# One 512-column product for the high and the low input, in the MLP and the retention query and key projections of a two-block network

## The chip, the core and the metric

The kernel runs on one core of one Trainium2 chip. The metric is the device time of one execution in microseconds; the median of a few executions is compared.

## The reference

The reference passes 256 tokens of width 1024 through two blocks. The first has an even layer (windowed attention with sinks, heads "A", and neighbourhood attention, heads "B"), an MLP, a retention layer (8 heads, decays in both directions, a group norm per head) and another MLP. An MLP is `square(relu(rmsnorm(x) @ w1)) @ w2` with 4096 hidden columns. The second block has causal, top-k and cross attention with gates; the keys and values of its cross attention come from a second input `mem` (256 rows). Everything is float32:

```
def _mlp(x, norm_g, w1, w2):
    h = _rmsnorm(x, norm_g)
    return jnp.square(jax.nn.relu(h @ w1)) @ w2
# retention, one direction
    a = jnp.einsum('bhid,bhjd->bhij', qc, kc) * dmask
    o = jnp.einsum('bhij,bhjv->bhiv', a, vc) + ...
    yn = (yf - mu) * lax.rsqrt(var + GN_EPS) * gn_g
```

## The kernel before

**Split products.** A float32 product is made of three products in the format `fp32r`: a high part times a high part, high times low, low times high (`mm3`, L382 to L384). For the weights, ScalarE (ACT) copies each half tile of the weights to its high part `whi` (L904), and VectorE (DVE) subtracts it from the raw tile to get the low part `wlo` (L1297). There are six `whi` and five `wlo` buffers and four raw tiles of 1 MB, filled by SyncE's queue (SP) in the order of `weight_tiles()`. Each engine casts a fixed number of halves ahead (`HI_AHEAD` 5, `LO_AHEAD` 4), at places in its program that `used(...)` fixes. Each engine runs its own program in a hand-written order, so an operation that waits holds all behind it.

**Two forms of product.** `n_half` holds the input (tokens) stationary and streams 512 weight columns. `t_half` holds a 128x128 block of weights stationary and streams the 256 tokens, so the result comes out transposed: for each of 8 k-blocks of one half tile there are three 256-column matmuls, `whi` with `hTh`, `whi` with `hTl`, `wlo` with `hTh`. One PSUM bank of 512 columns takes both halves of a tile. `t_first` does the same for the first tile of a stage, in two banks, with transposes of the second half of the input put between.

**Where `t_half` is used.** The MLP's first product ("w1", 16 tiles in each of 2 layers), the retention's queries and keys ("rq", 8 tiles), and, untouched by the change, "xk", "xq", the gates "gl" and the up products "wu".

**MLP.** In step j PE does the two halves of w1 tile j, and then tile j-1 of the second product (`acc_half`, L456: 24 matmuls of 512 columns into four banks). Between them stands a chain: ACT takes relu from the bank (L1104; L1109 for the two banks of tile 0), DVE squares (L1620), ACT copies the high part (L1114), DVE subtracts for the low part (L1622). PE waits for the last, one step later.

**Retention.** `hTh`, `hTl` are the gained but not yet row-scaled inputs. The row scale 1/rms(x) of queries and keys is spread over the partitions by a matmul with a matrix of ones (`broadcast("ret")`, L542) and multiplied in as DVE empties the banks (L1650, L1646). The group norm adds `GN_EPS` on GpSimd (POOL).

**The first stage (about the first 140 us).** The order of the weight tiles is qa, ka, qb, kb, memT (the transposed `mem`, split on the spot with its gain, L899 and L1290), vb, xk, xv, oe. Attention steps `att_step("AB", s)` for s from 0 to 18 are interleaved with the product halves: scores (L553), on DVE scores plus bias (L1396 for A) and row maxima, exp on ACT (L989), transposes (L565), copies (L1428 DVE, L1002 ACT), values (L582). Queries and keys are normed (`hn_squares`, `hn_sums`, `hn_scales` on POOL, `hn_scaled` L1325) and transposed (L525). Row squares of x (L913) and of `mem` are taken by ACT.

Of the kernel before, what the change touches and what calls it, by code (L numbers as in the profile page):

```python
# [25 lines left out]
C_ID, C_NA, C_CA, C_COS, C_SIN, C_U, C_L, C_IS, C_NS = (  # L26
    0, 128, 640, 896, 1024, 1152, 1536, 1920, 1928)
NCONST = 1936
# [6 lines left out]
        "w0", "w1", "w2", "w3", "w4", "raw0", "raw1", "raw2", "raw3", "x0", "x1", "t0", "t1", "t2", "t3", "t4", "id", "c", "g", "b", "m", "out"]  # L35
# [17 lines left out]
def weight_tiles():  # L53
# [86 lines left out]
def program(nc, A, out):  # L140
    with ExitStack() as st:
# [7 lines left out]
        hTh, hTl = sb("hTh", 2048, F32R), sb("hTl", 2048, F32R)  # L149
# [69 lines left out]
        hT = (v3(hTh, 8), v3(hTl, 8))  # L219
        ur = [(v3(h, 4, 0, 1024), v3(l, 4, 0, 1024)) for h, l in zip(urh, url)]  # L220
        ones, diag, rbc = cst[:, C_U:C_U + 128], cst[:, C_U + 128:C_U + 384], cst[:, C_L:C_L + 256]
        spread = {"mem": (av(EO, 128), av(ED, 256), av(EB, 256)), "ret": (ones, diag, rbc), "sec": (ones, diag, rbc)}
# [5 lines left out]
        invs, negs = cst[:, C_IS:C_IS + 8], cst[:, C_NS:C_NS + 8]  # L228
        skp, hb = lgt[:, 0:8], lgt[:, 8:32]
# [83 lines left out]
        def sp_program(e):  # L313
# [6 lines left out]
            for m, (label, name, k0, nk, c0, n, _) in enumerate(tiles):  # L320
# [22 lines left out]
                if m == 3:  # L343
                    e.dma_start(cst[:, 128:NCONST], A["consts"][:, 128:NCONST]).then_inc(S["c"], 16)
                    e.dma_start(rows[:, :], bass.AP(A["rowvec"].tensor, 0, [[0, 128], [1, NROW]])).then_inc(S["c"], 16)
# [14 lines left out]
        def pe_program(e):  # L360
# [64 lines left out]

            def t_first(label, stage, between):


                i = first_half[label]
                w2 = [weights(i), weights(i + 1)]  # L430
                o = [take("mm", label, m) for m in range(2)]
                for g in range(2):
                    for m in range(2):
                        h, l = w2[m]
                        for k in range(4 * g, 4 * g + 4):
                            w.wait_ge(*at(*x_split(stage, k)))
                            mm = mm3(o[m][:, 0:256], (h[:, k, :], l[:, k, :]), (hT[0][:, k, :], hT[1][:, k, :]),
                                     k == 0, k == 7)
                        if g == 0 and m == 0:
                            between()  # L440
                        if g:
                            mm.then_inc(*up("mm", ("mm", label, m), ("wd", i + m)))
                            give("mm", label, m)
# [199 lines left out]
            for s in range(19):  # L643
                if s == 0:
                    n_half("kb", 0, 512, "E")
                    value["wd", first_half["memT"]] = value["wd", first_half["memT"] + 1] = value["wd", first_half["kb"]]
# [5 lines left out]
                if s < 3:  # L652
                    n_half("kb", s + 1, 512, "E")
                if s == 3:
                    hn_transposed("qb")
                if s == 6:
                    hn_transposed("kb")
                if 3 <= s < 7:
                    n_half("vb", s - 3, 512, "E")
                if s == 7:  # L660
                    broadcast("mem")
# [7 lines left out]
                if s >= 15:  # L669
                    i, x = (s - 15) // 2, (s - 15) % 2  # L670
                    if s == 15:
                        acc_open("E")
                    w.wait_ge(*at("xl", "oe", i))
                    acc_half("E", ("oe", i), x, hT, 2 * i, start=s == 15)
            for i in range(2, 4):
                transposes(("oe", i), osb, 2 * i, [("o", "B", 0), ("o", "B", 1)])
# [6 lines left out]
            def mlp(layer, before):  # L683
                t_first(("w1", layer, 0), f"mlp{layer}", lambda: x_transposed(f"mlp{layer}", before, (2, 3)))
                for j in range(17):
                    if j == 1:
                        acc_open(f"mlp{layer}")
                    if 1 <= j < 16:
                        for x in range(2):
                            t_half(("w1", layer, j), x, 256, 8, hT, lambda k: x_split(f"mlp{layer}", k))  # L690
# [15 lines left out]
            for c in range(8):  # L706
                for x in range(2 if c else 0):
                    t_half(("rq", c), x, 256, 8, hT, lambda k: x_split("ret", k))
                if c == 1:
                    broadcast("ret")  # L710

            def ret_scores(h):
                b = take("rs", h)
                w.wait_ge(*at("rq", 7))
# [163 lines left out]
        def act_program(e):  # L878
# [31 lines left out]
            def row_squares(stage, src, junk, needs):  # L910
                for tb in range(2):
# [63 lines left out]
            def att_exp(key, i):  # L975
# [8 lines left out]
                for j, h in enumerate(hs):  # L984
                    if key == "A":
                        scl, nm = 2.0 ** -(h + 1), stats(("nm", "A", qb), 8)[:, h:h + 1]
# [18 lines left out]
            def att_step(key, s):  # L1005
# [3 lines left out]
                if key == "AB" and s in (6, 10):  # L1009
                    sink_exp((s - 6) // 4)  # L1010
                if s < n:
# [37 lines left out]
            used("qa", 2)  # L1049
# [11 lines left out]
            for s in range(19):  # L1061
                att_step("AB", s)
                if s < 3:
                    used("kb", s + 1)
                if s == 3:
                    hn_stored("qb")
                    hn_squares("kb")
                if s == 4:
                    row_squares("mem", osb, osb, [(S["m"], 16), (S["m"], 16)])
                if s == 6:  # L1070
                    hn_stored("kb")
                if 3 <= s < 7:
                    used("vb", s - 3)
                if s == 7:
                    v_stored("vb", 0, 512, bvv[:, 1, :], "E")
                    stored_broadcast("mem")
# [14 lines left out]

            def mlp(layer, gcol, before):
# [3 lines left out]
                for j in range(17):  # L1096
                    if j < 16:
# [4 lines left out]
                        if j:  # L1102
# [945 lines left out]
```

## Time and profile before

| | |
|---|---|
| time, median of 3 | 1023.01 us (1022.87 to 1023.74) |
| profiled execution, its own time | 1024.58 us |
| its span in the trace | 1022.8 us |
| PE busy | 1002.8 us (98%), 6194 matmuls |
| PE weight loads busy | 892.1 us (87%), 6194 loads |
| DVE busy | 648.6 us (63%) |
| ACT busy | 488.3 us (48%) |
| POOL busy | 137.8 us (13%) |
| mean granted TensorE clock | 0.999 |

Engines: PE is TensorE's matmuls, PEld its weight loads, DVE VectorE, ACT ScalarE, POOL GpSimd, SP SyncE. A matmul's duration in a row includes its way through the array and overlaps the next one's, so the pace of a stream is read from start to start.

### The profile page before, as it was taken

The page shows a single profiled execution, that of the slowest core. Times are in us where ns is not written, and L with a number is a line of the kernel's source. Part 1 is how long each engine was busy: PE and PEld are TensorE (multiplying, and loading weights), DVE is VectorE, ACT ScalarE, POOL GpSimd, SP SyncE. Part 2 cuts the span into 40 slices and gives each one's busy share as a digit, 9 for nine tenths or more (in the row PEclk, how much of TensorE's full clock was granted, in tenths as well). Part 3 has the DMA queues.
Part 4 walks back from the last instruction along what each step waited for, and adds up shares of the span by engine and source line. Part 5 has one row for each costly group of instructions (what it writes and reads, how often), then busy time and mean ns, then how long its engine had stood idle before and what let it go on. Part 6 is the DMA issues. An engine that isn't in the chain of part 4 may idle for free.

```text
span 1022.8 us, 15392 instructions
## 1 busy us (share of the span) xinstructions
PE 1002.8 (98%) x6194; PEld 892.1 (87%) x6194; DVE 648.6 (63%) x916; ACT 488.3 (48%) x746; POOL 137.8 (13%) x173
## 2 busy tenths in 40 slices
PE   8889999999999999999999999999999999999997
PEld 7668879999998998888889999999887889999995
DVE  4687756664555655666666554455767887657674
ACT  5575536444554533234545444454545445545452
POOL 0631004970000200110001000000550110000000
PEclk9999999999999999999999999999999999999999
DMA  9963345465456544335464456545544463354541
GB/s 343 295 206 124 103 145 165 171 207 199 165 190 211 176 166 165 124 124 206 165 206 163 167 178 215 183 166 172 197 168 141 133 190 124 124 165 125 173 157 42
DMA packets 106933, 174.82 MB, mean 171 GB/s; under 512 B 4080, under 2 KB 66672, under 8 KB 106864
## 3 DMA queue, kind: packets, MB, share of 16 engines
q1 hardware_dynamic: 106144, 173.01, 50.9%
q8 instruction: 50, 0.82, 0.3%
q10 hardware_dynamic: 720, 0.83, 0.2%
q14 instruction: 19, 0.16, 0.0%
HBM read 172.79 MB, written 1.05 MB: 170 GB/s over the span
## 4 chain that ended last, share of the span: by engine, by line
PE 91%; DMA 3%; DVE 3%; SPq 1%; issue 1%; POOL 1%; ACT 1%; DVEq 0%; POOLq 0%
PE ps L456 23%; PE ps L382 20%; PE ps L384 19%; PE ps L383 19%; PE ps L582 2%; DMA raw<-in_memT 2%; PE ps L553 1%; PE ps L508 1%; PE ps L728 1%; PE ps L565 1%; DMA raw<-in_w_in_e 1%; PE ps L716 1%; DVE wlo L1297 0%; DVE arena L1396 0%; PE ps L535 0%
## 5 line engine op out<-in xcount | busy, mean ns | idle before, releaser
L1297 DVE TENSOR_TENSOR wlo<-raw,whi 128x1024 fp32r<-128x1024 f32 x314 | 373.8, 1229 | 30.3 <-ACT whi L904 13.9
L904 ACT ACTIVATE whi<-raw 128x1024 fp32r<-128x1024 f32 x314 | 317.4, 1049 | 95.5 <-PE ps L384 50.5
L382 PE MATMUL ps<-hTh,whi 128*128 128x256 f32 (+1 forms) x872 | 249.1, 286 | 0.4
L384 PE MATMUL ps<-hTh,wlo 128*128 128x256 f32 (+1 forms) x872 | 246.8, 283 | 0.0
L383 PE MATMUL ps<-hTl,whi 128*128 128x256 f32 (+1 forms) x872 | 246.8, 283 | 0.0
L382 PEld LDWEIGHTS ps<-hTh,whi 128*128 128x128 f32 (+1 forms) x872 | 166.8, 191 | 3.9 <-issue 1.9
L383 PEld LDWEIGHTS ps<-hTl,whi 128*128 128x128 f32 (+1 forms) x872 | 166.8, 191 | 1.2
L384 PEld LDWEIGHTS ps<-hTh,wlo 128*128 128x128 f32 (+1 forms) x872 | 166.8, 191 | 0.0
L382 PE MATMUL ps<-whi,hTh 128*128 128x512 f32 (+1 forms) x376 | 150.7, 401 | 6.3 <-DVE wlo L1297 2.3
L384 PE MATMUL ps<-whi,hTl 128*128 128x512 f32 (+1 forms) x376 | 145.3, 386 | 0.0
L383 PE MATMUL ps<-wlo,hTh 128*128 128x512 f32 (+1 forms) x376 | 145.1, 386 | 0.0
L456 PE MATMUL ps<-whi,urh 128*128 128x512 f32 x328 | 102.1, 392 | 0.0
L456 PE MATMUL ps<-wlo,urh 128*128 128x512 f32 x328 | 101.6, 390 | 0.0
L456 PE MATMUL ps<-whi,url 128*128 128x512 f32 x328 | 101.5, 390 | 0.0
L1620 DVE TENSOR_TENSOR arena<-arena 128x512 f32<-128x512 f32 x32 | 22.8, 713 | 122.7 <-ACT arena L1104 122.4
L382 PEld LDWEIGHTS ps<-whi,hTh 128*128 128x128 f32 x376 | 70.8, 188 | 24.4 <-issue 7.5
L384 PEld LDWEIGHTS ps<-whi,hTl 128*128 128x128 f32 x376 | 70.8, 188 | 14.8
L383 PEld LDWEIGHTS ps<-wlo,hTh 128*128 128x128 f32 x376 | 71.0, 189 | 12.9
L1104 ACT ACTIVATE arena<-ps 128x512 f32<-128x512 f32 x30 | 17.9, 598 | 131.8 <-PE ps L384 131.8
L456 PEld LDWEIGHTS ps<-wlo,urh 128*128 128x128 f32 x328 | 61.6, 188 | 13.1
L456 PEld LDWEIGHTS ps<-whi,url 128*128 128x128 f32 x328 | 61.6, 188 | 13.0
L456 PEld LDWEIGHTS ps<-whi,urh 128*128 128x128 f32 x328 | 59.5, 189 | 10.4
(185 smaller groups left out, 1131.7 us busy)
## 6 DMA issues: line engine op xcount, KB each, us to landing
raw<-in_w SPq DMA_DIRECT2D x64, 1024.0 KB, 5.4
raw<-in_w_in SPq DMA_DIRECT2D x34, 1024.0 KB, 5.2
raw<-in_w_in_o SPq DMA_DIRECT2D x24, 1024.0 KB, 5.4
raw<-in_w_out_o SPq DMA_DIRECT2D x8, 1024.0 KB, 5.0
raw<-in_w_in_e SPq DMA_DIRECT2D x7, 1024.0 KB, 14.5
raw<-in_w_mem SPq DMA_DIRECT2D x4, 1024.0 KB, 7.0
raw<-in_w_out_e SPq DMA_DIRECT2D x4, 1024.0 KB, 4.9
raw<-in_w_out SPq DMA_DIRECT2D x4, 1024.0 KB, 5.2
```

Source lines behind the costliest of these rows:

```text
L382: e.matmul(o, a[0], b[0], start=start, stop=False)
L383: e.matmul(o, a[0], b[1], start=False, stop=False)
L384: return e.matmul(o, a[1], b[0], start=False, stop=stop)
L456: mm = e.matmul(bank("acc", stage, 2 * tb + i), x[p], t[p % 2][:, 0, 512 * i:512 * i + 512], start=start and p == 0, stop=stop and p == 2)
L508: mm = e.transpose(b[:, j * 256 + tb * 128:j * 256 + tb * 128 + 128], src[:, tb, (k0 + j) * 128:(k0 + j) * 128 + 128], ident)
L553: mm = e.matmul(b[:, j * 256:j * 256 + nk], q_of(h, qb), k_of(h, nk), start=True, stop=True)
L565: mm = e.transpose(b[:, (j * nb + kb) * 128:(j * nb + kb) * 128 + 128], P[:, j, kb * 128:kb * 128 + 128], ident)
L582: mm = e.matmul(b[:, h * hd:h * hd + hd], T[:, (j * nb + kb) * 128:(j * nb + kb) * 128 + 128], v_of(h, kb), start=kb == 0, stop=kb == nb - 1)
L904: e.activation(split_half(i)[0], raw_half(i), ACT.Copy).then_inc(*up("hi", ("hi", i)))
L1104: e.activation(rl, bank("mm", ("w1", layer, j), 0), ACT.Relu).then_inc(*up("aev", ("rl", layer, j), ("free", ("mm", ("w1", layer, j), 0))))
L1297: e.tensor_tensor(l, raw_half(i), h.bitcast(F32), ALU.subtract).then_inc(*up("lo", ("lo", i)))
L1620: e.tensor_tensor(sq, rl, rl, ALU.mult).then_inc(*up("dst", ("sq2", layer, j)))
```

## The change

1. `hTh` and `hTl` become one buffer in which, for each k-block, 256 high columns stand beside 256 low ones. In "w1" and "rq", `t_pair` replaces the two `t_half`: per k-block one matmul of `whi` with all 512 columns and one of `wlo` with the 256 high ones. Each half tile now fills a whole bank: columns 0 to 255 hold high times high plus low times high, 256 to 511 high times low.
2. ACT copies the right half of the bank out (`low_copied`), DVE adds the left half to it (`low_added`), for each half tile. In the MLP, relu and square become one DVE operation.
3. The retention's broadcast goes away. The keys' scale is applied as a per-row factor to the scores (`rk`), the queries' is left out, and the group norm's epsilon is scaled to match (`ge`).
4. The first stage is reordered: weight tiles vb before memT, `weights_to(6)` and the row squares of x ahead of weight halves 6 and 7, the rest of the constants and of the row vector loaded at tile 14 in place of tile 3, `mem`'s row squares one per step, its broadcast at s = 9, "xk" emptied at s = 10 and 12, the last two "oe" transposes at s = 18 inside the loop; `used(...)` before the norm work in DVE's and ACT's steps. The A heads' sink maximum and scale become one DVE operation in place of two.

```
-        hTh, hTl = sb("hTh", 2048, F32R), sb("hTl", 2048, F32R)
+        hTs = sb("hT", 4096, F32R)
+        h4 = hTs[:, :].rearrange("p (k s n) -> p k s n", k=8, s=2)
+        hT = (h4[:, :, 0, :], h4[:, :, 1, :])
...
+    rows_first("vb", "w_in_e", 1792, 512)
     rows_first("memT", "memT", 0, 256)
-    rows_first("vb", "w_in_e", 1792, 512)
...
-                if m == 3:
-                    e.dma_start(cst[:, 128:NCONST], A["consts"][:, 128:NCONST]).then_inc(S["c"], 16)
-                    e.dma_start(rows[:, :], ...).then_inc(S["c"], 16)
+                if m == 4:
+                    e.dma_start(cst[:, 128:C_COS], A["consts"][:, 128:C_COS]).then_inc(S["c"], 16)
+                    e.dma_start(rows[:, R_SINK:NROW], ...).then_inc(S["c"], 16)
+                if m == 14:
+                    e.dma_start(cst[:, C_COS:NCONST], A["consts"][:, C_COS:NCONST]).then_inc(S["c2"], 16)
+                    e.dma_start(rows[:, 0:R_SINK], ...).then_inc(S["c2"], 16)
...
+            def t_block(label, m, ks, stage):
+                i = first_half[label] + m
+                h, l = weights(i)
+                o = bank("mm", label, m)
+                for k in ks:
+                    w.wait_ge(*at(*x_split(stage, k)))
+                    both = hTs[:, k * 512:k * 512 + 512]
+                    if k == 0:
+                        e.matmul(o, h[:, k, :], both, start=True, stop=False)
+                    mm = e.matmul(o[:, 0:256], l[:, k, :], hT[0][:, k, :], start=False, stop=False)
+                    if k:
+                        mm = e.matmul(o, h[:, k, :], both, start=False, stop=k == 7)
+                if k == 7:
+                    mm.then_inc(*up("mm", ("mm", label, m), ("wd", i)))
+                    give("mm", label, m)
...
+            def low_copied(label, m, dst):
+                w.wait_ge(*at("mm", label, m))
+                e.activation(dst, bank("mm", label, m)[:, 256:512], ACT.Copy).then_inc(*up("aev", ("lc", label, m)))
...
+            def low_added(label, m, d):
+                w.wait_ge(*at("lc", label, m))
+                e.tensor_tensor(d, bank("mm", label, m)[:, 0:256], d, ALU.add).then_inc(
+                    *up("dev", ("t", label, m), ("free", ("mm", label, m))))
...
-                        e.tensor_tensor(sq, rl, rl, ALU.mult).then_inc(*up("dst", ("sq2", layer, j)))
+                        w.wait_ge(*at("t", ("w1", layer, j), 1))
+                        e.scalar_tensor_tensor(sq, rl, 0.0, rl, ALU.max, ALU.mult).then_inc(*up("dst", ("sq2", layer, j)))
...
-            used("qa", 2)
+            weights_to(6)
             row_squares("E", x3, osb, [(S["x0"], 16), (S["x1"], 16)])
```

## Rows read from the trace of the kernel before

**Rows 1.** The page: busy time per engine; DMA share and rate in 40 slices.
```profile
PE 1002.8 (98%) x6194; PEld 892.1 (87%) x6194; DVE 648.6 (63%) x916; ACT 488.3 (48%) x746; POOL 137.8 (13%) x173
...
DMA  9963345465456544335464456545544463354541
GB/s 343 295 206 124 103 145 165 171 207 199 165 190 211 176 166 165 124 124 206 165 206 163 167 178 215 183 166 172 197 168 141 133 190 124 124 165 125 173 157 42
```
**Rows 2.** The page, the chain that ended last, shares of the span.
```profile
PE 91%; DMA 3%; DVE 3%; SPq 1%; issue 1%; POOL 1%; ACT 1%; DVEq 0%; POOLq 0%
```
**Rows 3.** The chain that ended last, in order: start, length, work (us).
```profile
164.89 5.47 PE ps L456 x24
...
321.97 5.47 PE ps L456 x24
...
346.79 0.45 PE ps L542 x2
```
**Rows 4.** Timeline of PE where 512-column and 256-column matmuls meet (start, us).
```profile
304.38 0.62 PE L456 MATMUL ps<-whi,url 128*128 128x512 f32 x2
304.83 0.28 PE L382 MATMUL ps<-hTh,whi 128*128 128x256 f32 x1
304.94 0.28 PE L383 MATMUL ps<-hTl,whi 128*128 128x256 f32 x1
305.06 0.28 PE L384 MATMUL ps<-hTh,wlo 128*128 128x256 f32 x1
...
310.46 0.28 PE L384 MATMUL ps<-hTh,wlo 128*128 128x256 f32 x1
310.58 0.63 PE L456 MATMUL ps<-whi,urh 128*128 128x512 f32 x2
311.05 0.62 PE L456 MATMUL ps<-wlo,urh 128*128 128x512 f32 x2
```
**Rows 5.** Groups by line and shape: busy us, mean ns, idle before, releaser.
```profile
L1620 DVE TENSOR_TENSOR arena<-arena 128x512 f32<-128x512 f32 x32 | 22.8, 713 | 122.7 <-ACT arena L1104 122.4
L1622 DVE TENSOR_TENSOR url<-arena,urh 128x512 fp32r<-128x512 f32 x32 | 22.2, 694 | 22.3 <-ACT urh L1114 22.3
L1114 ACT ACTIVATE urh<-arena 128x512 fp32r<-128x512 f32 x32 | 20.2, 632 | 26.6 <-DVE arena L1620 26.6
...
L1104 ACT ACTIVATE arena<-ps 128x512 f32<-128x512 f32 x30 | 17.9, 598 | 131.8 <-PE ps L384 131.8
...
L1109 ACT ACTIVATE arena<-ps 128x256 f32<-128x256 f32 x4 | 1.3, 398 | 0.0
...
L1646 DVE TENSOR_TENSOR arena<-ps,cst 128x256 f32<-128x256 f32 x2 | 0.8, 420 | 2.3 <-ACT cst L972 2.3
```
**Rows 6.** Timeline of PE, 28 to 90 us, matmuls that waited (brackets).
```profile
29.38 0.47 PE L382 MATMUL ps<-whi,hTh 128*128 128x512 f32 x1 [0.70 <-DVE wlo L1297]
...
34.51 0.66 PE L525 MATMUL ps<-cst,arena 128*128 128x128 f32 x4 [1.70 <-DVE arena L1325]
...
51.95 0.66 PE L565 MATMUL ps<-cst,arena 128*128 128x128 f32 x4 [0.41 <-ACT arena L989]
...
60.29 0.47 PE L382 MATMUL ps<-whi,hTh 128*128 128x512 f32 x1 [1.48 <-DVE arena L1396]
...
66.66 0.47 PE L382 MATMUL ps<-whi,hTh 128*128 128x512 f32 x1 [1.02 <-DVE wlo L1297]
...
75.84 1.11 PE L582 MATMUL ps<-arena 128*128 128x64 f32 x8 [1.65 <-ACT arena L1002]
...
84.17 0.36 PE L382 MATMUL ps<-urh,whi 128*128 128x256 f32 x1 [0.59 <-DVE arena L1396]
```
**Rows 7.** Timeline of ACT in the first stage: start, length, work, wait.
```profile
23.19 1.04 ACT L913 ACTIVATE arena<-xs 128x1024 f32<-128x1024 f32 x1
...
49.21 1.71 ACT L899 ACTIVATE urh<-raw,gain 128x256 fp32r<-128x256 f32 x4 [5.66 <-DMA raw<-in_memT]
```
**Rows 8.** DMA issues by line: KB each, median us from issue to landing.
```profile
raw<-in_memT SPq DMA_DIRECT2D x1, 1024.0 KB, 17.0
```

More of the change, by code:

```diff
@@ L424, in t_half, with t_pair @@
                         mm.then_inc(*up("wd", ("wd", i)))
-            def t_first(label, stage, between):
[L429 to L443, printed above, removed]
+            def t_block(label, m, ks, stage):
[13 more added lines that the diff above has]
+                    give("mm", label, m)
+            def t_pair(label, stage):
+                for m in range(2):
+                    take("mm", label, m)
+                    t_block(label, m, range(8), stage)
+            def t_first(label, stage, between):
+                for m in range(2):
+                    take("mm", label, m)
+                    t_block(label, m, range(4), stage)
+                    if m == 0:
+                        between()
+                for m in range(2):
+                    t_block(label, m, range(4, 8), stage)
             def acc_open(stage):
@@ L672, in pe_program @@
                         acc_open("E")
+                    if s == 18:
+                        for k in range(2, 4):
+                            transposes(("oe", k), osb, 2 * k, [("o", "B", 0), ("o", "B", 1)])
                     w.wait_ge(*at("xl", "oe", i))
                     acc_half("E", ("oe", i), x, hT, 2 * i, start=s == 15)
-            for i in range(2, 4):
-                transposes(("oe", i), osb, 2 * i, [("o", "B", 0), ("o", "B", 1)])
             w.wait_ge(*at("xl", "oe", 2))
@@ L688, in mlp @@
                     if 1 <= j < 16:
-                        for x in range(2):
-                            t_half(("w1", layer, j), x, 256, 8, hT, lambda k: x_split(f"mlp{layer}", k))
+                        t_pair(("w1", layer, j), f"mlp{layer}")
                     if j >= 1:
@@ L705, in pe_program @@
             t_first(("rq", 0), "ret", lambda: x_transposed("ret", "mlp0", (2, 3)))
[L706 to L710, printed above, removed]
+            for c in range(1, 8):
+                t_pair(("rq", c), "ret")
             def ret_scores(h):
                 b = take("rs", h)
-                w.wait_ge(*at("rq", 7))
+                w.wait_ge(*at("t", ("rq", 7), 1))
                 for jb in range(2):
@@ L908, in used, with row_squares @@
                 weights_to(first_half[label] + j + HI_AHEAD)
-            def row_squares(stage, src, junk, needs):
-                for tb in range(2):
+            def row_squares(stage, src, junk, needs, blocks=range(2)):
+                for tb in blocks:
                     w.wait_ge(*needs[tb])
@@ L1010, in att_step @@
                     sink_exp((s - 6) // 4)
+                if key == "AB" and s in (4, 5):
+                    row_squares("mem", osb, osb, [(S["m"], 16), (S["m"], 16)], (s - 4,))
                 if s < n:
@@ L1101, in mlp @@
                             w.wait_ge(*at("sq2", layer, j - 2))
[L1102 to L1110 removed]
+                        for m in range(2):
+                            low_copied(("w1", layer, j), m, rl[:, m * 256:m * 256 + 256])
                         w.wait_ge(*at("sq2", layer, j))
@@ L1133, in act_program @@
             row_squares("ret", x3, av(OY, 2048, 2), [at("x", "mlp0", 1), at("x", "mlp0", 3)])
-            used(("rq", 1), 1)
-            stored_broadcast("ret")
-            used(("rq", 7), 1)
+            for c in range(8):
+                used(("rq", c), 1)
+                for m in range(2):
+                    low_copied(("rq", c), m, (oqT if c < 4 else okT)[:, 2 * (c % 4) + m, :])
             for c in range(4):
@@ L1301, in used, with row_reciprocals @@
                 weights_to(first_half[label] + j + LO_AHEAD)
-            def row_reciprocals(stage):
-                for tb in range(2):
+            def row_reciprocals(stage, blocks=range(2)):
+                for tb in blocks:
                     i = stats(("i", stage, tb), 1)
@@ L1575, in dve_program @@
                 att_step("AB", s)
+                if s < 3:
+                    used("kb", s + 1)
+                if 3 <= s < 7:
+                    used("vb", s - 3)
+                if 7 <= s < 11:
+                    used(("xk", (s - 7) // 2), (s - 7) % 2)
                 if s == 1:
                     hn_scaled("qb")
-                if s < 3:
-                    used("kb", s + 1)
                 if s == 3:
```

109 lines of the change are left out of this document (44 added, 65 removed).

## The prediction

> **What bounds the kernel now.** I read the busy shares first, then the chain that ended last, then PE's own timeline for what is left. PE is busy for 98% of the span, DVE for 63% [rows 1], and 91% of the chain is PE's work [rows 2]. The reader is to see that between about 85 us and the end PE sets the time: whatever shortens PE's stream there shortens the kernel, and whatever is added to DVE or ACT costs only what comes out from under PE. Fourteen steps of the first MLP, between the starts of the second product at 164.89 and 321.97, take 157.08 us, 11.22 us each [rows 3], evenly and with no wait in them. Only the first stage has waits on PE: seven of some size between 28 and 85 us, 0.70 + 1.70 + 0.41 + 1.48 + 1.02 + 1.65 + 0.59 = 7.6 us [rows 6]. There the DMA engines' share is at its highest too (the first two slices are 9 tenths or more, the third 6 [rows 1]; a slice is 25.6 us).
>
> **The pace of a matmul.** Two matmuls of 512 columns take 0.45 us from start to start at 304.38 and 0.47 at 310.58; one of 256 takes 0.11 right behind a 512 one and 0.12 in the steady stream [rows 4]. Out of a whole step: 24 x 0.227 = 5.45 us for the second product, and the remaining 5.77 us over 48 matmuls of 256 columns are 0.120 us each. So 512 columns cost less than twice 256 columns (0.227 against 0.240): each matmul carries about 13 ns that don't depend on its columns.
>
> **1. The products.** A k-block (I call it a unit) changes from three matmuls of 256 to one of 512 and one of 256: the columns stay 768, one matmul and one weight load go. Units: 2 halves x 8 = 16 per tile, 32 tiles of w1 and 8 of rq, so 640. A unit now takes 3 x 0.120 = 0.360 us. The trace has no stream that alternates 512 and 256, so the new unit is bounded by the two seams of [rows 4]. Lower bound: a 256 one behind a 512 one at 0.11 plus 0.227 is 0.337. Upper bound: the 512 one behind a 256 one at 0.235 (half of 0.47) plus 0.120 is 0.355. The gain per unit is 5 to 23 ns. I take the plain sum between them, 0.227 + 0.120 = 0.347, since the two seams together (0.11 + 0.235 = 0.345) come to the same. That is 13 ns x 640 = **8.3 us**, with 3.2 and 14.7 us as ends.
>
> This can be weighed against the Trainium skill ("TensorE: Matmul & The Clock Gate", Back-to-back issue gap), which gives a matmul of N columns at full clock N/2.4 ns plus 2.5. By that rule a unit goes from 327.5 to 325 ns, and the estimate for 640 units is only 1.6 us. The rows show 120 and 227 ns where the rule has 109 and 216, so the trace does not agree with it here, and the sum goes by the rows.
>
> **2. Emptying the banks in the MLP.** Per step ACT does two copies of 256 columns (2 x 398 ns by L1109) in place of one relu (598), and DVE adds two additions of 256 columns (2 x 420, by L1646) and one square of about the old 713 ns [rows 5]. That is +0.2 us on ACT and +0.85 us on DVE per step. DVE now waits 122.4 us over 32 steps for ACT, 3.8 us each, and ACT 131.8 over 30, 4.4 us each [rows 5]: room for both. The chain behind the last half of a tile was 598 + 713 + 632 + 694 ns = 2.6 us; it becomes 398 + 420 + 713 + 632 + 694 = 2.9 us, some 3.3 with one more semaphore. PE wants its result a whole step later (11 us; for tile 0 only the next tile's 5.6 us). The weight halves queued behind it on DVE and ACT are cast four and five ahead, 2.8 us of PE time each, so 0.5 us later is hidden. Each tile now holds two banks for one; beside the four accumulators four remain, used again two tiles (22 us) later. Cost: nothing. If the cover were gone, it would be the 0.5 us per step, 16 us in all.
>
> **3. Retention.** The broadcast matmul leaves PE, 0.45 us [rows 3]. Two 256-column additions replace one 512-column multiplication per tile on DVE, two copies per tile come to ACT; both have only two casts per 5.6 us of PE there. POOL loses the two diagonal products and gets about a dozen tiny operations, of which one addition per head stands in the norm chain; DVE waits for it, PE doesn't until the head's bank is wanted again. Cost: nothing, up to 0.2 us x 8 = 1.6 us if it showed. Gain **0.5 us**.
>
> **4. The first stage.** ACT stands 5.66 us at 49.21 for memT, which landed 17.0 us after its issue; the exp of the first scores is queued behind it [rows 7, 8], and DVE's part of memT follows. With vb first, ACT's cast comes as soon as that tile lands, one operation of about 1 us in place of four (1.71), and about 1 MB of constants and row vector no longer stand ahead of it: at the 295 to 343 GB/s of the first two slices [rows 1] that is about 3 us. Wait by wait [rows 6]: the 0.70 at 29.38 comes from ACT's squares (23.19 [rows 7]) standing ahead of weight half 7 and goes; of the 1.70 at 34.51 POOL's chain remains, 0.3 goes; the 0.41 at 51.95 is the exp behind memT and goes; the 1.48 at 60.29 is a bank that a late DVE empties, 1.2 goes; the 1.02 at 66.66 is a cast behind the key norms, which now stands ahead of them: 1.0 goes; the 1.65 at 75.84 is ACT's copy behind both row squares of mem, now one per step, 1.0 goes; of the 0.59 at 84.17, 0.4. Sum 5.0 us. What is late next is DVE itself: between 57 and 80 us it gets memT's low part, the key norm and the A scores, so I keep 0.3 us of the smaller edits (one operation less in each A unit, the seam of the oe transposes, which wait for the last values instead of waiting later) out as a plus only: **5.3 us**. Ends: 1 us (the waits move on to DVE) and 7.6 us (all of them go). The moved DMAs: SP issues two more at tile 14, where the share is 3 to 4 tenths [rows 1]; nobody waits for them before the decays and the ropes.
>
> **Sum.** 8.3 + 0.5 + 5.3 = 14.1 us. The profiled execution took 1024.6 us, 1.8 more than its span of 1022.8 and 1.6 more than the median shown; against its own time the sum gives 1010.5, against the median 1023.0 it gives **1008.9 us**.
>
> **Rivals.**
> A. The 13 ns are not saved by a shorter list of matmuls: the alternation runs at the seam pace, 0.354 per unit, or the weight load that follows a 256-column matmul sets the pace. For: the loads are busy 87% of the span [rows 1]. Against: both streams show the same 13 ns. Gain 3.8 + 0.5 + 5.3: 1013.4 us. (The page's rule, in its own sentence, would end at 1023.0 - 1.6 - 5.8 = 1015.6.)
> B. The first stage gives nothing: DVE takes over as releaser of the same banks. For: it is DVE that is named in five of the seven waits [rows 6]. Gain 8.8: 1014.2 us.
> C. The alternation is at its low end and the first stage sheds all: 14.7 + 0.5 + 7.6: 1000.2 us.
> D. Slower: the copy-add handshake of tile j holds DVE and ACT so that weight halves come late in each MLP step. It decides once the chain is longer than the some 7 us at which the second half of the next w1 tile is wanted, 5.5 + 2.8 less one cast; it is about 3.3. At 0.6 us lost per step over 30 steps, 18 us, the gain is gone: 1027 us.
> E. The change does what it says but a bank wait eats it in the first stage and at the seams of the MLPs: about no change, 1022 us.
>
> **How the numbers follow.** The forecast (gain 10 to 18 us, 1005 to 1013) 0.60; A 0.12; B 0.12; C and between 0.08; D 0.05; E 0.03. The likeliest time is 1009 us, its own range 1005 to 1013. The range for 8 in 10 takes in A and nearly B at one end and half of C at the other: 1003.5 to 1015.5. About 0.2% (2 us) is what a measurement of this kernel can tell from no change. Faster by more than that: forecast, A, B, C, 0.92; within 0.03; slower 0.05.
>
> **What would show it.** The step in the MLP falls from 11.22 to 5.45 + 16 x 0.347 = 11.0 us, and the starts of a 512 and the next unit's 512 matmul are 0.347 us apart; 640 fewer matmuls, 6194 less 640 and the broadcast's two, 5552 of both kinds. The first 256-column matmul of xk starts near 78 us, not 84.17. PE has no wait within the MLPs; DVE's idle time ahead of the square falls but stays above 2 us a step. I am wrong if a unit takes 0.355 or more, if PE waits for DVE in the MLP, or if xk starts after 82 us.

## The result, and the profile after

The changed kernel takes 1014.69 us (median of 4, 1012.75 to 1016.23), the kernel before 1023.31 beside it: a ratio of 0.9916 with the interval 0.9904 to 0.9928. It is faster by 8.6 us. The forecast was 14.1 us faster, 1008.9 us; the time lies in the range for 8 in 10 (1003.5 to 1015.5) and outside the likeliest one (1005 to 1013). The profiled execution took 1014.96 us, with a span of 1013.2 us and a mean granted clock of 0.995 (0.999 before).

The page: busy time of each engine, then two of the rows in 40 slices. They answer to [rows 1].

```profile
PE 997.9 (98%) x5552; PEld 858.6 (85%) x5552; DVE 676.3 (67%) x979; ACT 496.7 (49%) x791; POOL 131.8 (13%) x175
...
PEclk9989999999999999999999999999999999999999
DMA  9954345556566554425465566555544354444541
```

There are 642 matmuls and as many loads fewer, 5552, as the prediction had it, and DVE has 28 us more work. In the third slice (51 to 76 us) the granted clock is below nine tenths; the prediction puts no price on a fall of the clock.

The chain that ended last, in order: start, length, work. It answers to [rows 3].

```profile
147.34 0.87 PE ps L525 x8
...
162.40 5.46 PE ps L473 x24
173.45 5.44 PE ps L473 x24
...
316.88 5.44 PE ps L473 x24
```

The second products of the same fourteen steps now start 316.88 - 162.40 = 154.48 us apart, 11.03 us each instead of 11.22. The first row is where the first MLP begins, with the transposes of its input. The same row of the kernel before, from its chain:

```profile
149.60 0.87 PE ps L508 x8
```

So the whole first stage brought this profile only 2.3 us. (Single profiles differ in their first 30 us whatever the order: the kernel x_prod below has the first stage of before and reaches the same matmul, the one at 29.38 in [rows 6], at 27.44. The medians of whole times are the safer measure.)

PE's timeline inside such a step (start, us), where [rows 4] had the three 256-column matmuls:

```profile
159.88 0.40 PE L441 MATMUL ps<-hT,whi 128*128 128x512 f32 x1
160.11 0.28 PE L439 MATMUL ps<-hT,wlo 128*128 128x256 f32 x1
160.23 0.40 PE L441 MATMUL ps<-hT,whi 128*128 128x512 f32 x1
160.47 0.28 PE L439 MATMUL ps<-hT,wlo 128*128 128x256 f32 x1
160.59 0.40 PE L441 MATMUL ps<-hT,whi 128*128 128x512 f32 x1
```

Two units go by from 159.88 to 160.59, 0.355 each as these rounded starts show it; out of the whole step a unit is (11.034 - 5.45) / 16 = 0.349 us, against 0.360 before. No row of PE within the MLPs has a wait of 0.2 us or more.

The groups by line that took the place of [rows 5]: busy us, mean ns, idle before, releaser.

```profile
L1628 DVE TENSOR_TENSOR arena<-ps,arena 128x256 f32<-128x256 f32 x80 | 33.3, 423 | 102.2 <-ACT arena L1110 101.7
L1110 ACT ACTIVATE arena<-ps 128x256 f32<-128x256 f32 x80 | 30.1, 384 | 131.8 <-PE ps L441 131.8
...
L1642 DVE SCALAR_TENSOR_TENSOR arena<-arena 128x512 f32<-128x512 f32 x32 | 22.9, 717 | 3.1
```

Addition, copy and square cost 423, 384 and 717 ns (forecast from neighbours: 420, 398, 713), and DVE and ACT still stand idle for over 100 us each (102.2 ahead of the additions, 131.8 ahead of the copies).

So the steps of the MLP did nearly what was forecast, and the shortfall is in the first stage. Its PE timeline, rows with a wait in brackets, from two stretches between 28 and 90 us (they answer to [rows 6]):

```profile
32.05 0.47 PE L384 MATMUL ps<-whi,hT 128*128 128x512 f32 x1 [0.24 <-DVE wlo L1311]
...
59.90 2.63 PE L570 MATMUL ps<-arena 64*128 64x256 f32 x8 [1.30 <-ACT arena L943]
...
79.08 0.36 PE L384 MATMUL ps<-urh,whi 128*128 128x256 f32 x1
...
85.49 1.14 PE L570 MATMUL ps<-arena 64*128 64x256 f32 x8 [2.02 <-DVE arena L1353]
```

All seven waits of before are gone or small, and xk starts at 79.08 instead of 84.17. But two waits are there that weren't, each ahead of scores (L570), each for a PSUM bank that another engine still holds. What those engines did meanwhile is in their own timelines, first ACT's:

```profile
56.61 1.69 ACT L913 ACTIVATE urh<-raw,gain 128x256 fp32r<-128x256 f32 x4
58.21 1.06 ACT L936 ACTIVATE arena<-ps 128x512 f32<-128x512 f32 x2
59.16 0.68 ACT L943 ACTIVATE arena<-ps,gain 128x512 f32<-128x512 f32 x1
```

L943 stores the transposed queries of qb and so frees the bank. It stands behind the high part of memT (L913) and the squares of kb (L936), which in the new order fall into the same step of ACT's program. DVE's timeline ahead of the second wait:

```profile
82.35 2.36 DVE L1311 TENSOR_TENSOR wlo<-raw,whi 128x1024 fp32r<-128x1024 f32 x2 [2.32 <-ACT whi L918]
84.63 0.16 DVE L1321 RECIPROCAL stat<-stat 128x1 f32<-128x1 f32 x1
84.70 0.73 DVE L1353 TENSOR_SCALAR arena<-ps,stat 128x512 f32<-128x512 f32 x1
```

L1353 empties the bank of vb. `used(("xk", 0), 0)`, which the change put ahead of it, makes the cast of a weight half come first that is wanted only four halves later, and the casts in this row wait 2.32 us for ACT. The cast ahead of its need holds back an evacuation that is needed now.

The third thing is the clock. Windows of 1 and 2 us around the first wait: busy time and count of PE, PEld, DVE, ACT, POOL, then the granted clock, DMA share, GB/s.

```profile
59.00:60.00 1.00, 0.10 (x1) 0.11 (x1) 1.00 (x2) 1.00 (x3) 0.31 (x2) 1.00 1.06 410
60.00:61.00 1.00, 1.00 (x5) 0.89 (x6) 0.70 (x2) 1.00 (x2) 1.00 (x1) 0.76 1.04 399
61.00:62.00 1.00, 1.00 (x5) 0.67 (x2) 0.57 (x2) 0.45 (x2) 0.90 (x2) 0.50 0.17 64
...
64.00:66.00 2.00, 2.00 (x6) 1.55 (x5) 1.97 (x5) 1.82 (x6) 0.95 (x3) 0.50 0.00 0
66.00:68.00 2.00, 2.00 (x9) 1.58 (x8) 1.97 (x7) 0.00 (x0) 0.00 (x0) 0.66 0.00 0
68.00:70.00 2.00, 2.00 (x15) 1.82 (x14) 1.05 (x2) 1.80 (x4) 0.00 (x0) 1.00 0.31 67
```

PE is nearly idle (0.10 us of 1, most of the rest being the wait) at 59 us, then the granted clock falls from 1.00 to 0.50, that is from 2.4 to 1.2 GHz, and comes back at about 67.4 us. In 6.8 us at half speed PE does the work of 3.4, so this costs up to 3.4 us more than the wait itself; where PE would have waited further on anyway, less. In its profile the kernel before has no such stretch between its start and its last few microseconds.

The theory at this point: the products give about 7.4 us (11.6 ns x 640) and the first stage little, because two evacuations stand late in ACT's and DVE's orders and the waits they make pull the clock down. The rivals: the seams between the two widths eat part of the products' gain; the longer chain behind each half tile costs something; the new order of the loads is at fault.

### The profile page after: what moved, and what is told of

The parts are those of the page before. It is cut to its first block, busy times and chain, and to the rows that moved or that the text cites. A ratio compares the mean times of both kernels' runs of the same rounds, so it can differ in the third digit from the quotient of the medians.

```text
span 1013.2 us, 14176 instructions
## 1 busy us (share of the span) xinstructions
PE 997.9 (98%) x5552; PEld 858.6 (85%) x5552; DVE 676.3 (67%) x979; ACT 496.7 (49%) x791; POOL 131.8 (13%) x175
## 4 chain that ended last, share of the span: by engine, by line
PE 92%; DMA 3%; DVE 2%; SPq 1%; ACT 1%; issue 1%; POOL 0%; DVEq 0%; POOLq 0%
PE ps L473 24%; PE ps L441 13%; PE ps L384 13%; PE ps L386 12%; PE ps L385 12%; PE ps L439 7%; DMA raw<-in_w_in_e 3%; PE ps L599 2%; PE ps L438 2%; PE ps L570 2%; PE ps L525 2%; PE ps L742 1%; PE ps L582 1%; PE ps L730 1%; PE ps L552 0%
## 5 line engine op out<-in xcount | busy, mean ns | idle before, releaser
L441 PE MATMUL ps<-hT,whi 128*128 128x512 f32 x560 | 200.0, 396 | 0.0
L439 PE MATMUL ps<-hT,wlo 128*128 128x256 f32 x640 | 166.0, 280 | 0.0
L384 PE MATMUL ps<-whi,hT 128*128 128x512 f32 (+1 forms) x376 | 151.4, 403 | 2.5 <-DVE hT L1567 1.9
L386 PE MATMUL ps<-whi,hT 128*128 128x512 f32 (+1 forms) x376 | 146.0, 388 | 0.0
L385 PE MATMUL ps<-wlo,hT 128*128 128x512 f32 (+1 forms) x376 | 145.8, 388 | 0.0
L439 PEld LDWEIGHTS ps<-hT,wlo 128*128 128x128 f32 x640 | 120.6, 188 | 8.2 <-DVE hT L1363 1.0
L441 PEld LDWEIGHTS ps<-hT,whi 128*128 128x128 f32 x560 | 105.1, 188 | 21.2
L1628 DVE TENSOR_TENSOR arena<-ps,arena 128x256 f32<-128x256 f32 x80 | 33.3, 423 | 102.2 <-ACT arena L1110 101.7
L1110 ACT ACTIVATE arena<-ps 128x256 f32<-128x256 f32 x80 | 30.1, 384 | 131.8 <-PE ps L441 131.8
L384 PEld LDWEIGHTS ps<-whi,hT 128*128 128x128 f32 x376 | 71.2, 189 | 21.0 <-issue 6.1
L386 PEld LDWEIGHTS ps<-whi,hT 128*128 128x128 f32 x376 | 71.2, 189 | 15.0
L385 PEld LDWEIGHTS ps<-wlo,hT 128*128 128x128 f32 x376 | 71.4, 190 | 13.2
L473 PEld LDWEIGHTS ps<-whi,urh 128*128 128x128 f32 x328 | 61.4, 188 | 11.6
L384 PE MATMUL ps<-hT,whi 128*128 128x256 f32 (+1 forms) x232 | 66.8, 288 | 0.0
L386 PE MATMUL ps<-hT,wlo 128*128 128x256 f32 (+1 forms) x232 | 65.6, 283 | 0.0
```

The source lines that it names most:

```text
L384: e.matmul(o, a[0], b[0], start=start, stop=False)
L385: e.matmul(o, a[0], b[1], start=False, stop=False)
L386: return e.matmul(o, a[1], b[0], start=False, stop=stop)
L439: mm = e.matmul(o[:, 0:256], l[:, k, :], hT[0][:, k, :], start=False, stop=False)
L441: mm = e.matmul(o, h[:, k, :], both, start=False, stop=k == 7)
L473: mm = e.matmul(bank("acc", stage, 2 * tb + i), x[p], t[p % 2][:, 0, 512 * i:512 * i + 512], start=start and p == 0, stop=stop and p == 2)
```

## The experiments

The times of the kernel before beside the experiments are 1023.11, 1022.97 and 1023.35 us (medians of 13, 7 and 7).

### The two halves of the change by themselves

x_prod is the kernel before with parts 1 to 3 of the change; x_front is the kernel before with part 4.

```
x_prod:  before + hTs, t_block/t_pair, low_copied/low_added, rk and ge in place of broadcast("ret")
x_front: before + tile order, weights_to(6), DMAs at tile 14, mem's squares per step,
         broadcast("mem") at s == 9, oe transposes at s == 18, used(...) first
```

> The new products and the retention scale alone (parts 1 to 3 of the change), with the first stage of the kernel before. Theory (parts add up): a unit costs 0.3505 us in place of 0.360, so 640 x about 10.7 ns = 6.9 us, and 0.45 us for the broadcast: 7.3 us less than before, about 1015.9 us, the clock at 0.999 with no fall before the end, the waits between 28 and 85 us as before. Rival (the reordered first stage is what gives the gain): 3 us less or fewer.

> The reordered first stage alone (part 4), with the products of before. Theory (the new wait of PE near 59 us leads to the fall of the clock, and the two eat most of the part's gain): the MLP of layer 0 starts 2.3 us earlier than before, 1.0 to 3 us less time than before (about 1021 us), and the clock is at half speed for some 7 us from about 60.5 us, mean 0.995 to 0.996. Rival (the fall belongs to the new products): no half-speed stretch, and 5 us less than before.

x_prod takes 1016.36 us, a ratio of 0.9939 (0.9924 to 0.9954); x_front 1022.04 us, 0.9989 (0.9980 to 0.9998). The products are worth 6.8 us by themselves, the first stage 1.1 (x_front had been expected to gain 1.0 to 3). The profiles can be cut where the stages begin: from the transposes of the first MLP to those of the retention, from there to the second MLP, and so on, each stage is

| kernel | first MLP begins | first MLP | retention | second MLP |
|---|---|---|---|---|
| before | 149.6 us | 181.91 | 204.15 | 181.91 |
| after | 147.3 | 179.07 | 202.51 | 179.09 |
| x_prod | 150.4 | 179.07 | 202.51 | 179.03 |
| x_front | 147.3 | 181.91 | 204.14 | 181.91 |

The products give 2.84 + 1.64 + 2.82 = 7.3 us with either first stage, and the first MLP begins at 147.3 us with either kind of product once the first stage is reordered. x_front's PE timeline has the two new waits too, with the old products:

```profile
61.54 1.70 PE L554 MATMUL ps<-arena 64*128 64x256 f32 x8 [2.39 <-ACT arena L931]
...
85.53 1.14 PE L554 MATMUL ps<-arena 64*128 64x256 f32 x8 [2.02 <-DVE arena L1342]
```

So it is the reordering that makes them, not the wider products.

The falls of the clock are another matter. x_prod was expected to have none, and its profile has two, with the old order of the first stage: 3.4 us at half speed from 33.9 us, behind the wait of 1.74 us, and 6.8 us from 74.8, behind the one of 1.64.

```profile
34.00:36.00 2.00, 2.00 (x5) 1.59 (x6) 2.00 (x3) 0.54 (x1) 2.00 (x1) 0.50 1.12 207
76.00:78.00 2.00, 2.00 (x10) 1.19 (x9) 1.67 (x5) 0.36 (x2) 1.85 (x5) 0.50 0.19 23
```

Set beside the profile of before, which has the same waits without a fall, this also prices them. x_prod is 1.9 us ahead of it at the third marked wait (33.82 against 35.73), 1.6 ahead at the last one (74.27 against 75.84) and 0.8 behind where the first MLP begins. So the first fall cost 0.3 us of the 1.7 that it could, the second 2.4 of 3.4.

### ACT's order repaired (x_qb)

```
-                if 3 <= s < 7:
-                    used("vb", s - 3)
                 if s == 3:
-                    hn_squares("kb")
                     hn_stored("qb")
+                    hn_squares("kb")
+                if 3 <= s < 7:
+                    used("vb", s - 3)
```

> The changed kernel with ScalarE's step 3 put back as it was before: the queries of B are stored, then the keys squared, then the next weight half cast. Theory: the 1.30 us wait at 59.9 us goes, and with it the fall of the clock, which costs 3.4 us (6.8 us at half speed): 4 to 5 us less than the changed kernel, about 1010.2 us, mean clock 0.999. Rival (the fall is due to the mix of work in that stretch and not to the wait): only 0.5 to 1.3 us less, the half-speed stretch stays.

1011.94 us (1011.4 to 1015.29), a ratio of 0.9900 (0.9880 to 0.9921); this interval overlaps that of the changed kernel, and the 1010.2 us expected were not reached. The wait at 59.90 is gone and the clock stays at 1.00 there. The wait for vb's bank is longer, and half speed follows it. PE's timeline of x_qb:

```profile
81.33 1.82 PE L570 MATMUL ps<-arena 64*128 64x256 f32 x8 [3.04 <-DVE arena L1353]
```

The windows behind it, with columns as above:

```profile
80.00:82.00 2.00, 0.67 (x4) 0.65 (x6) 1.88 (x4) 0.06 (x1) 1.14 (x5) 0.91 1.02 416
82.00:84.00 2.00, 2.00 (x10) 1.28 (x8) 0.80 (x2) 0.00 (x0) 1.22 (x2) 0.50 1.01 395
84.00:86.00 2.00, 2.00 (x15) 2.00 (x15) 2.00 (x3) 1.39 (x5) 0.00 (x0) 0.73 0.63 256
```

PE is ready for this bank at 78.3 (81.33 less the wait), 5.2 us earlier than the changed kernel (83.5), while DVE frees it only some 4.2 us earlier, and the difference is the longer wait. One repair was not enough.

### The idle time filled, the wait left (x_fill)

```
+                    if label == "vb" and j == 0 and tb == 0:
+                        for r in range(6):
+                            e.matmul(o, xT[0][:, 0, 0:128], h[:, 0, :], start=True, stop=True)
```

> The changed kernel with six repeated 512-column matmuls (1.36 us) put in front of the first half of vb, some 5 us ahead of the wait; the results don't change. Theory (the idle time of PE leads to the fall): the repeats take the place of the 1.30 us wait, the clock stays up, and the kernel is about 3.4 us faster than the changed one (1011.3) though PE does more. Rival (the fall doesn't hang on the idle time): half-speed stretch as before it, time unchanged or up to 1.4 us longer.

1013.01 us (1012.78 to 1013.17), 0.9903 (0.9888 to 0.9918): by the medians 1.7 us faster than the changed kernel, with more work on PE and nothing else repaired, though the two intervals overlap. No wait and no fall of the clock at 60 us any more; from 83.2 on, behind the wait for vb's bank (1.96 us), there are 3.4 us at half speed, which the changed kernel doesn't have there:

```profile
81.94 1.14 PE L573 MATMUL ps<-arena 64*128 64x256 f32 x8 [1.96 <-DVE arena L1356]
```

```profile
84.00:86.00 2.00, 2.00 (x11) 2.00 (x11) 2.00 (x3) 1.45 (x5) 0.00 (x0) 0.50 0.97 352
```

Against 6.8 us at half speed in the changed kernel that is 3.4 less, worth up to 1.7 us, as much as the medians differ by. The 3.4 us expected came by half, since the clock fell elsewhere. Work of 1.36 us put into idle time of PE lengthened nothing.

### Both orders repaired (x_both)

x_qb, and in DVE's program

```
+                if s == 7:
+                    row_reciprocals("mem", (1,))
+                    v_stored("vb", bvv[:, 0, :], "E")
                 if 7 <= s < 11:
                     used(("xk", (s - 7) // 2), (s - 7) % 2)
...
-                if s in (6, 7):
-                    row_reciprocals("mem", (s - 6,))
-                if s == 7:
-                    v_stored("vb", bvv[:, 0, :], "E")
+                if s == 6:
+                    row_reciprocals("mem", (0,))
```

> The kernel with ScalarE's step 3 put back, and besides VectorE's step 7 with vb's values stored ahead of the cast of the xk half (as before the change). Theory (what is left of the reorder's loss is the bank that vb's late evacuation holds, because VectorE waits for ScalarE's casts first): the 3.04 us wait at 81.33 us of the kernel with the first repair falls to under 0.5 us, no half-speed stretch there, about 2 to 3 us less than that kernel (1009 to 1010 us), MLP of layer 0 starts near 142 us. Rival (the weight casts are themselves what PE waits for, the data coming late): the wait stays as a wait for wlo, less than 0.7 us gained.

1007.14 us (1007.0 to 1007.79), a ratio of 0.9846 (0.9831 to 0.9861): the fastest kernel of the study, 15.8 us under the kernel before and 7.6 under the changed one. DVE's timeline of x_both:

```profile
74.45 0.73 DVE L1353 TENSOR_SCALAR arena<-ps,stat 128x512 f32<-128x512 f32 x1
```

PE's, the rows with a wait of any size up to the first MLP:

```profile
31.49 0.47 PE L384 MATMUL ps<-whi,hT 128*128 128x512 f32 x1 [0.27 <-DVE wlo L1311]
...
92.44 0.66 PE L582 MATMUL ps<-cst,arena 128*128 128x128 f32 x4 [0.41 <-DVE arena L1610]
...
126.25 1.09 PE L525 MATMUL ps<-cst,arena 128*128 128x128 f32 x8 [0.79 <-DVE arena L1467]
```

vb's bank is emptied at 74.45 instead of 84.70, and three small waits are left on PE. The first MLP begins at 139.6 us, 10.0 earlier than in the profile of before. The clock has no stretch at half speed ahead of the last few microseconds.

### DVE's order repaired alone (x_v)

> The changed kernel with the second repair only (VectorE's step 7, vb's values stored ahead of the weight cast). Theory (two waits, each with a cost of its own, the first with a fall of the clock behind it): the wait at 85 us goes, 2.0 us less than the changed kernel, about 1012.7 us; the wait near 60 us and the half-speed stretch stay; the rest to the kernel with both repairs (some 5.5 us) is the first wait's and the clock's. Rival (one repair does it all): near 1008 us.

1011.27 us, 0.9880 (0.9860 to 0.9901), and its four runs fall into two pairs: 1009.04 and 1009.58 us at a granted clock of 0.999, 1012.96 and 1013.24 at 0.996. The profile, of one of the slower pair, has the wait for ACT's store:

```profile
60.73 2.64 PE L570 MATMUL ps<-arena 64*128 64x256 f32 x8 [2.23 <-ACT arena L943]
```

Its windows show half speed behind the wait:

```profile
58.00:60.00 2.00, 0.49 (x5) 0.35 (x4) 0.35 (x1) 2.00 (x6) 0.00 (x0) 1.00 0.41 148
60.00:62.00 2.00, 1.27 (x5) 1.20 (x7) 1.53 (x3) 2.00 (x4) 1.48 (x2) 0.59 0.99 385
62.00:64.00 2.00, 2.00 (x8) 1.15 (x6) 1.13 (x3) 0.28 (x2) 1.73 (x4) 0.50 0.00 0
```

The faster pair has no trace; that its clock did not fall there is read from its mean alone. If so, the runs take the clock apart from the wait: the faster pair has a mean of 1009.3 us, 2.2 above x_both, as much as the wait (2.23), and the slower pair is 3.8 above the faster, near the 3.4 us that 6.8 us at half speed (from 60.4 us on) can come to. This is argued and not shown. The mean clock is a weak witness, since it also counts the half speed of the last microseconds, which lasts 2.3 to 4.4 us in the profiles. The kernel before has eight runs with a mean clock of 0.994 to 0.996 among the 27 beside the experiments, and they are only 0.6 us longer on average than the other nineteen; x_prod takes 1016.05 us at 0.995 and 1015.99 at 0.998.

### The old products with the repaired first stage (x_front_both)

```
x_front + the two repairs of x_both (t_half, mm3 and broadcast("ret") as before)
```

> The products of before, the reordered first stage, and both repairs in it. Theory (the parts add up): first stage 10 us shorter than before, 1013.1 us; against the kernel with both repairs it lacks the 7.3 us of the products (1014.4 by that difference), so 1013 to 1014.5. Rival (the repaired first stage gains only with the new products): over 1018 us.

1014.77 us (1014.6 to 1014.85), 0.9915 (0.9900 to 0.9930): the repaired first stage is worth 8.6 us without the new products. x_both is 7.6 under it, which is what the products are worth on top. The test of whether the two parts interact needs each of them alone: 6.8 (x_prod) + 8.6 = 15.4 us, against 15.8 measured for both. Each ratio is known to 0.15%, 1.5 us, and within that they add up.

### The constants early again (x_dma)

x_both, with the whole table of constants and the whole row vector loaded at tile 3:

```
-                if m == 4:
+                if m == 3:
                     e.dma_start(cst[:, 128:C_COS], ...)
...
-                if m == 14:
+                if m == 3:
                     e.dma_start(cst[:, C_COS:NCONST], ...)
```

> The kernel with both repairs, but with all the constants and the whole row vector loaded at tile 3 again. Theory (the 1 MB moved away brings vb's tiles 3 us earlier, and the exp of the first scores waits for them): ScalarE's wait for the DMA grows by 3 us and a wait of PE comes back near 50 us, 1 to 3 us more than with both repairs (1008 to 1010). Rival (moving the loads is worth nothing, the order of memT and vb does it): within 0.5 us of 1007.1.

1011.06 us, 0.9873 (0.9857 to 0.9890), 3.9 above x_both. ACT's timeline of x_dma:

```profile
47.57 1.06 ACT L918 ACTIVATE whi<-raw 128x1024 fp32r<-128x1024 f32 x1 [8.29 <-DMA raw<-in_w_in_e]
```

PE's timeline just behind it:

```profile
49.66 0.66 PE L582 MATMUL ps<-cst,arena 128*128 128x128 f32 x4 [3.34 <-ACT arena L1003]
```

The window:

```profile
52.00:54.00 2.00, 2.00 (x5) 1.61 (x6) 2.00 (x4) 1.53 (x5) 0.00 (x0) 0.50 1.05 378
```

In x_both the same cast of vb starts at 44.53 with a wait of 5.23 us. The tile lands 3 us later, as the prediction estimated for the constants; the exp queued behind the cast on ACT is late, PE waits 3.34 us for it, and 3.4 us at half speed follow. Loading the constants late is a sound part of part 4, worth a little more than the 1 to 3 us expected. What vb before memT is worth was not tested by itself; x_dma keeps that order.

### The order inside a half tile (x_order, x_best)

Each half tile does all products with `wlo` first and then all with `whi`, so that matmuls of one width stand together; x_order is the changed kernel with it, x_best is x_both with it.

```
                     mm = e.matmul(o[:, 0:256], l[:, k, :], hT[0][:, k, :], start=False, stop=False)
+                for k in ks:
                     if k:
                         mm = e.matmul(o, h[:, k, :], hTs[:, k * 512:k * 512 + 512], start=False, stop=k == 7)
```

> The changed kernel with all low products of a half tile issued together and then all products with the high weights: two seams between 256 and 512 columns per half tile (one per group in the first tile) in place of eight. Theory (the 0.3505 us of a unit are the plain 0.227 + 0.120 and 3.5 us per thousand units of seams): the unit falls to about 0.3475 us, an MLP step from 11.03 to 10.99 us, 1.5 to 2 us less than the changed kernel. Rival (the alternation costs nothing of its own): same time, step 11.03 us.

> Both repairs of the first stage and the grouped order of the products. Theory (the parts add up): 1.5 to 2 us less than the kernel with both repairs, about 1008 us. Rival: no further gain.

x_order takes 1016.96 us, 0.9936 (0.9919 to 0.9952), x_best 1008.78, 0.9863 (0.9848 to 0.9877): 1.6 us above x_both. The step of an MLP is 11.025 us against 11.034: the seams cost 9 ns in a step, nothing. The expectation of x_order is refuted. What is lost lies in the first tile of each of the three stages, 0.55 to 0.63 us a stage (the first MLP takes 179.64 us in x_best against 179.09 in x_both). There the transposes of the input arrive in pieces, and the grouped order wants the last of a group earlier: each of the three first tiles of x_best has a wait of 0.28 us that x_both doesn't have.

```profile
146.84 0.50 PE L438 MATMUL ps<-hT,wlo 128*128 128x256 f32 x2 [0.28 <-DVE hT L1363]
```

### A longer chain behind the bank (x_copies)

```
                 w.wait_ge(*at("mm", label, m))
+                if label[:2] == ("w1", 0):
+                    for r in range(3):
+                        e.activation(av(8192 + 256 * (3 * m + r), 256), bank("mm", label, m)[:, 256:512], ACT.Copy)
```

> The changed kernel with three more copies of the right half of each bank on ScalarE in the first MLP, ahead of the one that counts, into unused memory: 1.15 us more in the chain behind each half tile, 2.3 us more work of ScalarE per step. Theory (the emptying of the banks is hidden under PE, 11 us of cover): the step of the first MLP stays 11.03 us, time unchanged within 0.3 us. Rival (the handshake is close to the bound): the step grows, by up to 1.15 us x 15 = 17 us in all.

1016.32 us, 0.9929 (0.9914 to 0.9944), by the medians 1.6 us above the changed kernel, with intervals that overlap. The chain that ended last in x_copies:

```profile
163.25 5.52 PE ps L473 x24
174.35 5.44 PE ps L473 x24
...
306.75 5.44 PE ps L473 x24
```

From 174.35 to 306.75 there are twelve steps of 11.03 us, the same as without the copies. 3 x 384 ns = 1.15 us more in the chain behind each half tile cost 0.08 us once, at the first tile, and some 0.5 us at the end of the first MLP, where no step stands behind to cover it. The time was expected to be unchanged within 0.3 us; that held for the steps and not for this end. The rest of the 1.6 us is ahead of the first MLP, which begins 0.8 us later. The copies come only after that: there the wait for ACT's store is 2.38 us in this profile instead of 1.30, and the clock falls twice for 3.4 us, behind this wait and behind the one for vb's bank.

```profile
86.00:88.00 2.00, 2.00 (x11) 2.00 (x12) 1.97 (x3) 0.57 (x3) 0.69 (x2) 0.59 1.02 363
```

## Why the prediction was right and wrong

**The products (8.3 us forecast).** Right in kind, and the size nearly: 11.6 ns per unit in the steady step instead of 13, 7.4 us for 640; 7.3 us measured in the stages with the broadcast in it, 7.6 as x_both against x_front_both. The unit takes 0.349 us, between the 0.347 taken and the 0.355 named as the point of failure. (The 0.355 was no strict end: it halves 0.47 us over two matmuls, and with all of the seam put on the first it would be 0.243 + 0.120 = 0.363; rival A's sum uses 0.354. Nothing hung on it.) Rival A fell with that, and x_order shows why: there are no costly seams. The retention gave 1.64 us, 0.45 of it the broadcast's, so its units gave 9 ns each. By the formula of the Trainium skill ("TensorE: Matmul & The Clock Gate", Back-to-back issue gap) a unit would save 2.5 ns, and the runs show over four times as much; but the section gives it for an isolated matmul and says itself that a stream with a weight load for every matmul, which this kernel's is, runs at another pace. So the disagreement says that the formula doesn't fit this stream, not that it is wrong for its own case.

**Emptying the banks (nothing).** Right. PE never waits in the MLPs, the steps stayed equal with 1.15 us more in the chain, and DVE's idle time of 102.2 us over 80 additions, two to a tile, is 2.6 us per tile, above the 2 us that the prediction asked for (it now stands ahead of the additions and not of the square). Rival D had no footing.

**The retention's factors (0.5 us gained, up to 1.6 lost).** The broadcast's 0.45 us are in the stage's 1.64, and no wait of PE in that stage shows the norm chain.

**The first stage (5.3 us).** This is the step that failed: it gave 1.1 us (x_front) or, as the difference of the changed kernel and its products, 8.6 - 7.3 = 1.3. What it said of the seven waits came true: they went or shrank, and xk starts at 79.08 us (78 forecast, 82 the point of failure). But a sum over the waits that go is only a gain if none comes. The prediction named DVE as what is late next and took nothing off for it; it went through the moved loads and the queue behind the memT cast, and not through what else stands in ACT's step 3 and DVE's step 7. There, `used(...)` and with it memT's cast now stand ahead of two evacuations whose banks PE wants next, 1.30 + 2.02 us in the changed kernel. On top comes the fall of the clock, up to 3.4 us. Together that is up to 6.7 of the 7.6 us between the changed kernel and x_both; the rest was not separated. That the two orders cost the 7.6 us is shown by the edit that takes them back; how the sum divides into waits and clock is argued, as x_prod's falls cost 0.3 and 2.4 us of the 1.7 and 3.4 possible. Rival E had a bank wait in the first stage, but with a gain of 1 us for everything; rival B had nearly the result (1014.2 us), with DVE as the releaser, and that is half of it: the first of the two waits is ACT's. The total fell into the wide range because the products, the larger term, came out near their size.

**The upper end.** With the two orders repaired the first stage gives 8.6 us, more than the 7.6 held possible. The prediction's list had left out a wait of 0.57 us at 35.73 in the timeline of before and one of 0.98 at 139.78, and both are gone in x_both, which has only small ones of 0.41 and 0.79 us in their place; the small edits (an operation less in each A unit, the oe transposes inside the loop) were put at 0.3 us without a run.

## What to carry to other kernels

When work is reordered, the sum of the waits that go is an upper bound, if the list is complete; write down for each engine which evacuations stand behind the moved operations, and compare their new place with when PE wants the bank. An operation done ahead of its need (a weight cast four half tiles early) belongs behind one that frees a bank, not ahead of it. And in a part of a kernel where PE has gaps, look at the granted clock before and after: here a wait of 2.2 us came with 6 us more in two of four runs (x_v against x_both).

## What the runs showed of the hardware

**The clock falls behind short waits, and not always.** In the changed kernel a wait of 1.30 us is followed by 6.8 us at 1.2 GHz; in x_qb one of 3.04 us by 3.4 us, in x_dma one of 3.34 us by 3.4. In x_v, by the mean clocks, only two runs of four have the fall. The wait for vb's bank, 1.96 to 2.02 us, is followed by a fall in x_fill and x_copies and by none in the changed kernel and x_front. The kernel before has waits of 1.70, 1.48 and 1.65 us and no fall in its profile; x_prod, with waits of 1.74, 1.01 and 1.64, falls twice (3.4 us from 33.9 and 6.8 from 74.8). What decides between the two is left open. Nor is the price the same each time: the two falls of x_prod cost 0.3 and 2.4 us. The Trainium skill ("TensorE: Matmul & The Clock Gate", A second HAM failure mode: psum-queue depth-cycling) says that frequent short idle spells of TensorE, as it turns through PSUM banks, made its clock switch between the two levels in another kernel. The traces agree in part: the falls of the changed kernel and of x_qb stand behind bank waits, but behind a single one each, and x_dma's stands behind a wait for data (3.34 us for the exp).

**Width and pace.** A unit of one 512-column and one 256-column matmul in turn takes 0.349 us, and the same sixteen units with the widths grouped take no more or less; three of 256 columns take 0.360: what counted was the number of matmuls, about 12 ns for each one fewer, whatever stood beside it.
